# Starting every weight place and every rounded activation of a two-model kernel on a multiple of 128 bytes in SBUF

## The reference

```python
def swiglu(x, w_gate_up, w_down):
    gate, up = jnp.split(x @ w_gate_up, 2, axis=-1)
    return (jax.nn.silu(gate) * up) @ w_down

for l in range(DEPTH):
    x = x + FFN_HALF * swiglu(rms_norm(x, ffn1_norm[l]), ffn1_w_gate_up[l], ffn1_w_down[l])
    u = rms_norm(x, mix_norm[l]) @ w_in[l]
...
    x = x + y @ w_out[l]
    x = x + FFN_HALF * swiglu(rms_norm(x, ffn2_norm[l]), ffn2_w_gate_up[l], ffn2_w_down[l])
```

## Time and profile before

| | before |
|---|---|
| median of 3 runs | 3337.23 us (3336.71 to 3341.22) |
| the profiled execution, its span (no other time of its own is recorded) | 3336.7 us |
| TensorE busy | 3223.2 us, 97% |
| weight loads busy (beside the matmuls) | 2786.5 us, 84% |
| VectorE busy | 2015.3 us, 60% |
| ScalarE busy | 1300.0 us, 39% |
| DMA | 469.30 MB, mean 141 GB/s |
| mean granted TensorE clock | 0.988 of full speed |

### The profile page before, as it was taken

The page is one execution under the profiler, slowest core; times in us unless marked ns, Lnnn a source line. Parts: engine busy times, 40 slices in busy tenths (PEclk is TensorE's granted clock), DMA queues, the critical chain, the costliest instruction groups (busy, mean ns, idle before and its releaser), DMA issues.

```text
span 3336.7 us, 46055 instructions
## 1 busy us (share of the span) xinstructions
PE 3223.2 (97%) x19162; PEld 2786.5 (84%) x19162; DVE 2015.3 (60%) x2437; ACT 1300.0 (39%) x1566; POOL 116.0 (3%) x126
## 2 busy tenths in 40 slices
PE   7998998999999998999999999999999999999998
PEld 7988987998988888898788877888878788877897
DVE  5777657778776657678766744744343334444554
ACT  5444244544445244554322233312242233434443
POOL 0001200000000301000000000000000000000000
PEclk9999999999999999999999999999999999999999
DMA  6652022565563021466444521532222322332552
GB/s 242 242 201 72 28 99 83 201 239 225 225 242 106 28 74 63 172 251 265 152 161 150 181 86 51 202 133 101 95 101 83 101 95 76 123 101 101 196 184 94
DMA packets 84970, 469.30 MB, mean 141 GB/s; under 512 B 7717, under 2 KB 11525, under 8 KB 44058
## 3 DMA queue, kind: packets, MB, share of 16 engines
q1 hardware_dynamic: 77952, 451.44, 37.0%
q10 hardware_dynamic: 6810, 14.91, 1.3%
HBM read 465.23 MB, written 1.10 MB: 140 GB/s over the span
## 4 chain that ended last, share of the span: by engine, by line
PE 74%; DVE 15%; ACT 6%; DMA 2%; issue 1%; POOL 0%; DVEq 0%; ACTq 0%; SPq 0%; POOLq 0%
PE ps L100 73%; DVE lo L317 5%; ACT hi L311 3%; DMA raw<-in_ffn_w_gate_up 1%; DMA raw<-in_ffn_w_down 1%; DVE prod L461 1%; PE ps L519 1%; DVE m0restMs L1970 0%; DVE m1restMs L1970 0%; DVE xt L682 0%; DVE ct L682 0%; DMA raw<-in_ffn_gu 0%; DVE half00fin L680 0%; DVE f21rot L852 0%; ACT f21hf_h L830 0%
## 5 line engine op out<-in xcount | busy, mean ns | idle before, releaser
L317 DVE TENSOR_TENSOR lo<-raw,hi 128x2048 fp32r<-128x2048 f32 (+1 forms) x357 | 809.7, 2268 | 616.5 <-ACT hi L311 600.8
L311 ACT ACTIVATE hi<-raw 128x2048 fp32r<-128x2048 f32 (+1 forms) x357 | 676.5, 1895 | 606.2 <-PE ps L100 476.6
L461 DVE SCALAR_TENSOR_TENSOR prod<-raw,silb 128x1024 f32<-128x1024 f32 x288 | 352.8, 1225 | 16.8 <-ACT silb L447 1.6
L100 PE MATMUL ps<-half00hs,hi 128*128 128x512 f32 x672 | 208.3, 391 | 0.8 <-DVE lo L317 0.8
L100 PE MATMUL ps<-half10hs,hi 128*128 128x512 f32 x672 | 208.3, 391 | 0.8 <-DVE lo L317 0.8
L100 PE MATMUL ps<-half02hs,hi 128*128 128x512 f32 x672 | 208.0, 391 | 0.8 <-DVE lo L317 0.8
L100 PEld LDWEIGHTS ps<-half00hs,hi 128*128 128x128 f32 x672 | 125.9, 188 | 30.4 <-DVE lo L317 2.0
L100 PEld LDWEIGHTS ps<-half02hs,hi 128*128 128x128 f32 x672 | 126.0, 188 | 30.3 <-DVE lo L317 1.7
L100 PEld LDWEIGHTS ps<-half10hs,hi 128*128 128x128 f32 x672 | 125.9, 188 | 30.1 <-DVE lo L317 1.7
L100 PE MATMUL ps<-half02hs,lo 128*128 128x512 f32 x352 | 138.8, 394 | 0.0
L100 PE MATMUL ps<-half10hs,lo 128*128 128x512 f32 x352 | 138.6, 394 | 0.0
(11 more groups left out here) (898 smaller groups left out, 7773.4 us busy)
## 6 DMA issues: line engine op xcount, KB each, us to landing
raw<-in_ffn_w_gate_up SPq DMA_DIRECT2D x88, 1024.0 KB, 8.3
raw<-in_ffn_gu SPq DMA_DIRECT2D x88, 1024.0 KB, 4.9
raw<-in_ffn_w_down SPq DMA_DIRECT2D x85, 1024.0 KB, 5.0
raw<-in_ada_w SPq DMA_DIRECT2D x72, 1024.0 KB, 6.6
raw<-in_w_in_t SPq DMA_DIRECT2D x28, 1024.0 KB, 4.9
raw<-in_ret_w_in SPq DMA_DIRECT2D x24, 1024.0 KB, 4.8
raw<-in_w_out SPq DMA_DIRECT2D x16, 1024.0 KB, 4.9
raw<-in_w_in_n SPq DMA_DIRECT2D x12, 1024.0 KB, 4.9
```

Source lines behind the costliest of these rows:

```text
L100: return p().matmul(o, l, r, start=start, stop=stop, skip_group_check=True)
L311: a().activation(self.high(w), self.raw[self.place(r)][:, 0:width], ACT.Copy).then_inc(*a.mark(self.wac, w))
L317: v().tensor_tensor(self.low(w), self.raw[self.place(r)][:, 0:width], self.high(w).bitcast(F32), ALU.subtract).then_inc(*v.mark(self.wdv, w))
L461: v().scalar_tensor_tensor(out=K.prod, in0=w[:, m, :], scalar=1.0, in1=K.silb[:, n, :], op0=ALU.mult, op1=ALU.mult, accum_out=K.mods[:, l, ...
```

## The change

```diff
-END = 229344
+END = 229248
+LINE = 128
...
-        m = Map(nc, (nc.sbuf_base + 31) // 32 * 32)
+        m = Map(nc, (nc.sbuf_base + LINE - 1) // LINE * LINE)
         at = [m.at + 8192 * i for i in range(5)] + [END - 8192 * (2 + i) for i in range(RAW - 5)]
...
         self.prod = m.take("prod", 1024)
+        m.at = (m.at + LINE - 1) // LINE * LINE
         self.free, self.end = m.at, END
         self.hi.append(Map(nc, m.at).take("hi2", 2048, dt=F32R))
```

## The result

The changed kernel takes 3352.14 us (median of 5 runs, 3348.77 to 3356.16), the kernel before 3337.23 us (5 runs in the same comparison, 3335.51 to 3341.22). The ratio is 1.0039, with a 95% interval of 1.0028 to 1.005: slower, 14.9 us between the medians, with a mean granted TensorE clock of 0.988 in both profiled executions. The prediction said 3312, with a range that ended at 3350. Its sign was wrong.

A forecast was written before the change was run, and what follows sets the result against it. TensorE's matmuls were taken to bound f20, f11 and half12, splits and transfers f10 and f21. Terms of -7.4, -2, -1.5 and -14 summed to -25 us, giving 3312 us (-0.75%), range 3278 to 3350 us.

The forecast's parts named there:

- The stages that TensorE bounds: Feed-forward stages f20, f11 and half12, whose chain is one unbroken run of matmuls: time off each matmul comes off the end.
- a stationary operand off a line always costs some 0.21 us a tile: Read from f20's 256-column tiles: stationary operand off a 128-byte line costs 4.4 ns a matmul; on it, fast or slow.
- The three comparisons: 256-column tiles, gate against down tiles, and half02's first tile: a stationary operand off the line costs 3 to 4.5 ns.
- Rows 9: Half02's first tile, six matmuls in 1.39 us: 232 ns each, against 228.9 with the stationary operand on the line.
- Down projections and their kin, -14: 4535 matmuls with 512 columns, 189 pieces: -0.1 us each, -18 in all, a fifth hidden under VectorE or transfers.
- Gate and up with 512 columns, 0: 3384 matmuls, stationary operand already on a line: no change taken, bounds +14.6 us (down pace) and -44 us.
- The 256-column stages, -7.4, -2 and -1.5 for the mixers: f20, f11, half12: -7.4 us; f10 and f21: -2; mixer and retention projections: -1.5, from tiles going to 5.44 us.
- The moving operand on a line is the dear one: Rival, chance 0.14: gate tiles go to the down pace, +14.6 us, 256-column tiles to 5.65 or over, +10; 3362 us.
- The slow pace locks in: Rival, chance 0.16: with no place off a line all 256-column tiles take 5.65 us, +5.7, down pieces +3.3; 3346 us.
- The fourth rival: Rival, chance 0.12: the change does nothing for the pace, e.g. gains and losses cancel; 3337 us.

The follow-up runs named there:

- bursts: Kernel of matmuls only, 48 per tile in three-fold form, stationary and moving operands at every pair of offsets 0 to 224 bytes; 512 columns: 680 to 703 ns a triple.
- bursts with the parts apart: Matmul-only kernels with rounded part and correction at separate offsets, stationary first, then moving; begun after a 512-column tile at distance 0. Stationary apart: 340 to 360 ns, 256 columns.
- one layout that holds 340 in one stage and 353 in the next: All operands alike modulo 256, but moving activations of the 256-column feed-forward stages 64 bytes further: 3316.2 us, ratio 0.993 to the kernel before.
- The table: Paces by operand offsets from matmul-only kernels; 512 columns, moving minus stationary modulo 256: 680 ns a triple at 0, 686.5 at 64, 697 at 128, 700 at 192.
- the cell chosen from them: Changed kernel with rounded weights and corrections 128 bytes apart, activations placed for 340 ns a triple at 256 columns: 3339.14 us, ratio 0.9995 to the kernel before.

## Why the prediction was wrong

*What held.* The stages that TensorE bounds were the right ones: what its matmuls gained or lost in f20, f11 and half12 came out in the chain, 2 us each, though shorter waits in the second mixer and in f21 gave most of it back in f20's and f11's case. Elementwise work and transfers cost nothing at their new addresses: 2268 and 1894 ns a split, and 5.0 us from issue to landing for a 1 MB tile of `ffn_w_down`, before and after. And the places of the operands do set the pace, against the Trainium skill's rule that PE never waits on anyone (SBUF — State Buffer, "Who interferes with whom"), as the prediction took it: by it all bursts would have read alike, and they read 680 to 703 ns, the same instructions on other offsets.

*The step that failed* is the reading in which "a stationary operand off a line always costs some 0.21 us a tile". It took each operand's rest on division by 128 as what counts. The three comparisons behind it were true numbers with another cause. The 256-column tiles in hi2 were at 5.65 us or more since hi2 lay at distance 0 and its correction, in lo0 to lo4, at 64, a pair for which the bursts read 353 ns a triple. Gate tiles were quicker than down tiles since one lay at a distance of 64 and the other at 192. Rows 9, which I called "both 64 past" and took as evidence that the stationary side costs 3 ns, had only the rounded weight there, at distance 0; its correction lay at 64 from the activations, and the 512-column bursts with the parts apart give 693 to 694.5 ns a triple for that, 231 ns a matmul. I never had a pair of rows in which the distance was the same and the place was not.

From it came three terms:
- Down projections and their kin, -14: their pace is 232.61 ns before and 232.50 after. Nearly all went from 192 to 128, from 700 to 697 or 701, and what had been cheap in places 5 to 7 (some 693) and in part in hi2 was lost. The 6.7 us less in the total are fewer waits.
- Gate and up with 512 columns, 0 "because 231 to 233 is explained by the stationary side": +12 us. The prediction's upper bound for it, +14.6 from the down pace, was nearly right. This term makes most of the measured loss, since the second block, where these stages are, has 12.9 of the 14.2 us between the two profiled spans.
- The 256-column stages, -7.4, -2 and -1.5 for the mixers: +12 in TensorE's total, of which little reached the end. The quick pace never appears in them, since at a distance of 128 tiles take 356 to 360.

The rival "The moving operand on a line is the dear one" had both sizes, +14.6 and +10, and the wrong cause: with all of it 64 bytes off the line the loss stays. Its 3362 lacked the fewer waits. That its signs were right is luck of this layout. "The slow pace locks in" was half right: paces are states, and there is one layout that holds 340 in one stage and 353 in the next; but the measured tiles went past 353, and most of the loss is in the 512-column gates, where it saw no change. The fourth rival named the true mechanism in one clause, "what counts is how the two operands lie to each other", and priced it at nothing for want of asking what the new distance is. The figure of the Trainium skill's page TensorE: Matmul & The Clock Gate ("Wait — 56ns, not 53.3ns?"), 215.7 ns from start to start at 512 columns once warm, isn't reached by any layout here: the best was 226.7, a third of 680.

What stays open: why the distance counts. Weight loads are busy for 2801.5 us beside the matmuls of the changed kernel, so the two operands are read at the same time, and a collision of these reads is a guess that fits; no run here shows that it is reads which collide. Open too is what chooses between two paces at one layout. The traces show only that a change comes with a break. The table's 680 carried over everywhere and its 353 and 350 in most stages, but its 340 not.

## What to carry to other kernels

When a matmul's time is asked by where its operands begin, ask for the distance between the moving and the stationary one, modulo 256 bytes here, before any multiple: a common alignment to 128 left them half a period apart, near the slowest. Measure the table in bursts of the very form that the kernel uses, begin them from more than one state, after a wait too (all of mine with the parts apart began from one, and the cell chosen from them failed), and expect part of the gain back as waits on the next engine. A row's duration does not show any of it; starts do. And if two explanations of a pace differ only in "place" and "distance", shifting the whole map by half a step is one edit that tells them apart.

## What the runs showed of the hardware that I had not expected

- Split matmuls with 512 columns take 680 to 703 ns a triple by the operands' distance modulo 256, 3%, at a granted clock of 0.999 in the bursts: 62 of 64 pairs agree with the others at their distance. The minimum is at distance 0.
- With 256 columns distance 0 is among the slowest, 360 ns, and the quickest pace, 340, stands where one of rounded weight and correction is 64 and the other 192 past the moving operands. One distance isn't best for both widths.
- One layout can have two steady paces at 256 columns, 340 and 353 with the activations at 64, and each change between them came with a break in TensorE's work. A layout whose bursts ran at 340, all begun from one state, held 357 in three stages of the real kernel.
